# Work moved across the stage borders of a hybrid attention, state-space and expert layer: w_out split and step-size tables in the projections, the first head loaded there, one tile of mixing prepared instead of four

## The reference, cut to what matters

```
proj = x @ w_in                       # q k v | z | xs B C | dt, x: 1536 tokens x 1024
q, k = partial_rotary(q), partial_rotary(k)
attn = merge of dilated window attentions, by their log-sum-exps
xBC  = silu(centred_dwconv(xs B C))
dt   = softplus(dt + dt_bias); A = -exp(a_log)       # two directions, 8 heads each
y    = ssd_scan forward + ssd_scan backward + d_skip * xs
y    = rms_norm(y * silu(z)) * ssm_norm_w
x    = layer_norm(ALPHA * x + concat([attn, y]) @ w_out)
x    = layer_norm(ALPHA * x + expert_choice_ffn(x))  # 16 experts
```

## Time and profile before

| | us |
|---|---|
| median of 3 runs | 3694.23 (3691.44 to 3696.48) |
| the profiled execution | 3689.45 |
| its span, first to last instruction | 3687.6 |
| PE busy in it | 3435.1 |
| DVE, ACT, POOL busy | 2331.2, 1893.5, 409.3 |
| mean granted TensorE clock | 0.96 of full speed |

### The profile page before, as it was taken

How to read it: one execution, slowest core, us unless ns; L and a number is a source line. 1 busy time by engine, 2 the same in 40 slices (tenths; PEclk the granted TensorE clock), 3 DMA queues, 4 the chain that set the end, 5 groups by cost and what they waited for, 6 DMA issues and landing times. The chain is left out here.

```text
span 3687.6 us, 61850 instructions
## 1 busy us (share of the span) xinstructions
PE 3435.1 (93%) x20358; PEld 3124.9 (85%) x20358; DVE 2331.2 (63%) x3830; ACT 1893.5 (51%) x3320; POOL 409.3 (11%) x373
## 2 busy tenths in 40 slices
PE   8999699788939999999999999999999999999993
PEld 6888699566829899998989999898998989899992
DVE  6421067687657676666757667675776767667674
ACT  3222167342316565555656556565565656556564
POOL 0011064333200000000000000000000000000003
PEclk9999889898969999999999999999999999999997
DMA  4222353133327777767777777777777777677775
GB/s 165 77 66 74 85 143 99 43 110 110 128 75 233 236 230 236 237 213 232 235 222 233 234 235 221 235 235 218 236 230 221 232 239 235 217 234 224 237 234 184
DMA packets 240063, 699.41 MB, mean 190 GB/s; under 512 B 52960, under 2 KB 68608, under 8 KB 239520
## 3 DMA queue, kind: packets, MB, share of 16 engines
q1 hardware_dynamic: 225920, 648.13, 54.9%
q0 software_dynamic: 13056, 45.29, 4.8%
q10 hardware_dynamic: 864, 3.15, 0.2%
HBM read 642.89 MB, written 57.77 MB: 190 GB/s over the span
## 5 line engine op out<-in xcount | busy, mean ns | idle before, releaser
L1847 PE MATMUL moe_gu<-moe_xgT,moe_whi 128*128 128x384 f32 x5632 | 1634.4, 364 | 7.6 <-issue 3.6
L1979 DVE TENSOR_TENSOR moe_wlo<-moe_raw,moe_whi 128x1024 fp32r<-128x1024 f32 x1056 | 1290.3, 1223 | 484.0 <-ACT moe_whi L1933 483.4
L1848 PE MATMUL moe_gu<-moe_xgT,moe_wlo 128*128 128x192 f32 x5632 | 1414.1, 251 | 0.0
L1933 ACT CAST moe_whi<-moe_raw 128x1024 fp32r<-128x1024 f32 x1056 | 1106.1, 1048 | 443.9 <-PE moe_dnp L1863 389.1
L1848 PEld LDWEIGHTS moe_gu<-moe_xgT,moe_wlo 128*128 128x128 f32 x5632 | 1083.7, 192 | 0.4
L1847 PEld LDWEIGHTS moe_gu<-moe_xgT,moe_whi 128*128 128x128 f32 x5632 | 1065.2, 189 | 13.0 <-issue 4.9
L1940 ACT COPY moe_part<-moe_gu 128x384 f32<-128x384 f32 x352 | 168.7, 479 | 459.2 <-PE moe_gu L1848 459.2
L1985 DVE TENSOR_TENSOR moe_guv<-moe_gu,moe_part 128x384 f32<-128x384 f32 x352 | 196.3, 558 | 292.5 <-ACT moe_part L1940 292.5
L1812 POOL DMA_INDIRECT tmp_acc<-moe_og_s,moe_srow_s x16 | 25.7, 1608 | 2286.4 <-ACT moe_og_s L1965 2286.4
L1859 PE MATMUL moe_dns<-moe_whi,moe_hid 128*128 128x512 f32 x704 | 275.9, 392 | 0.0
L1862 PE MATMUL moe_dnp<-moe_whi,moe_hid 128*128 128x512 f32 x704 | 275.6, 392 | 0.0
(11 more groups left out here) (275 smaller groups left out, 4128.6 us busy)
## 6 DMA issues: line engine op xcount, KB each, us to landing
moe_raw<-in_w_ffn SPq DMA_DIRECT2D x1056, 512.0 KB, 4.1
prj_wraw<-in_w_in SPq DMA_DIRECT2D x12, 1024.0 KB, 5.4
att_raw<-tmp_qkT SPq DMA_DIRECT2D x32, 384.0 KB, 7.0
prj_share<-in_xT SPq DMA_DIRECT2D x6, 1024.0 KB, 10.4
tmp_qkT<-prj_share POOLq DMA_DIRECT2D x24, 256.0 KB, 2.7
ssd_xb<-tmp_xbc SPq DMA_DIRECT2D x12, 512.0 KB, 3.9
mix_rows<-in_x SPq DMA_DIRECT2D x12, 512.0 KB, 5.2
tmp_h<-mix_rows SPq DMA_DIRECT2D x12, 512.0 KB, 2.6
```

The source lines that it names most:

```text
L1847: pe.matmul(out[:, a, 0:2 * CAP], whi[c][:, j, :], x, start=(j == 0), stop=False)
L1848: mm = pe.matmul(out[:, a, 0:CAP], wlo[c][:, j, :], x[:, 0:CAP], start=False, stop=(j == KD - 1))
L1933: act.copy(whi[c][:], raw[c][:]).then_inc(hi_done, 1)
L1979: dve.tensor_tensor(wlo[c][:], raw[c][:], whi[c][:].bitcast(F32), ALU.subtract).then_inc(lo_done, 1)
```

## The change

In the projections Z becomes slice 4 and V slice 5. In the Z slice w_out is read in 16 parts of 128x512, split into a high and a low half by ACT and DVE, and both halves are stored to DRAM by SP; during the V slice the step-size tables are made; head 0's q and k are loaded into a tensor that all four stages share (`early`), in place of the weights' staging buffer. Attention gets head 0 from there: POOL copies k, ACT copies q and makes qc, DVE does both subtractions, and the DRAM copy of w_out is gone. The state-space stage starts its loop after three constants, and loads the high half of w_out at its end. Mixing loads the low half by eight transfers, has no splits of w_out, and prepares tile 0 alone before the first product; `gate`, `far` and `norm` run two tiles ahead, `backward` three, and `project` is cut into two halves with the next tile's `turn` between them.

```diff
-    XB, QK, V, Z = (0, 1), (2, 3), 4, 5
+    XB, QK, Z, V = (0, 1), (2, 3), 4, 5
+    def out_part(of, q):
+        k, n = q // (D // OUT_W), q % (D // OUT_W)
+        return of[P * k:P * k + P, OUT_W * n:OUT_W * n + OUT_W]
+    def out_parts(t):
+        return [q for q in (2 * t - 6, 2 * t - 5) if 0 <= q < OUT_PARTS]
+        wraw = res["early"][:, 0:KD * ZW].rearrange("p (k n) -> p k n", k=KD)
+        raw0 = res["early"][:, 0:2 * TOK].rearrange("p (n t) -> p n t", n=2)
+        wst = [m.sb(f"wst{s}", [P, OUT_W]) for s in range(2)]
+        osh = m.sb("osh", [P, OUT_W], F32R)
+        osl = m.sb("osl", [P, OUT_W], F32R)
```

SP in the projections, behind its last load of weights:

```diff
+            def out_load(q):
+                if q < OUT_PARTS:
+                    sp.dma_start(wst[q % 2][:], out_part(dram["w_out"], q)).then_inc(wst_in[q % 2], 16)
+            out_load(0)
+            out_load(1)
+            for q in range(OUT_PARTS):
+                sp.wait_ge(out_lo, q + 1)
+                sp.dma_start(out_part(dram["whi"], q), osh[:].bitcast(F32)).then_inc(out_out, 16)
+                sp.dma_start(out_part(dram["wlo"], q), osl[:].bitcast(F32)).then_inc(out_out, 16)
+                out_load(q + 2)
+            sp.wait_ge(w_lo, KD * NW)
+            for s in range(2):
+                sp.wait_ge(rows_out[s], 16 * NT + 16)
+            for n in range(2):
+                for half in range(2):
+                    sp.dma_start(raw0[HD * half:HD * half + HD, n, :], dram["qkT"][n * AW:n * AW + HD, :]).then_inc(raw0_in, 16)
```

PE in the projections:

```diff
+            def sums():
+                pe.wait_ge(const_in, 96)
+                pe.wait_ge(qkT_ready, 2 * NT)
+                pe.wait_ge(tables, 1)
+                for n, (of, off) in enumerate(((GT, 0), (LT, HEADS), (LE, 0), (GE, HEADS), (ONE, 0), (ONE, HEADS))):
+                    at = NT * HEADS * (n % 3)
+                    mm = pe.matmul(ps[:, BANKS + n // 3, at:at + NT * HEADS], tri[:, of, :], dtA[:, :, off:off + HEADS],
+                                   start=True, stop=True)
+                mm.then_inc(sums_mm, 1)
+                    if n == V and t == 6:
+                        sums()
```

ACT in the projections:

```diff
+            def out_high(q):
+                act.wait_ge(wst_in[q % 2], 16 * (q // 2) + 16)
+                if q:
+                    act.wait_ge(out_out, 32 * q)
+                act.copy(osh[:], wst[q % 2][:]).then_inc(out_hi, 1)
             for n in range(2, NW):
                 for t in range(NT):
-                    if n < Z and t == NT - 1:
+                    if n < NW - 1 and t == NT - 1:
                         for k in range(KD):
                             w_part(n + 1, k)
                     rows(n, t, 0)
...
                     if n == Z:
                         rows(n, t, 1)
+                        for q in out_parts(t):
+                            out_high(q)
+                    if n == V and t in (0, 1, 7):
+                        exponents(t)
```

DVE in the projections:

```diff
+            def out_low(q):
+                dve.wait_ge(out_hi, q + 1)
+                dve.tensor_tensor(osl[:], wst[q % 2][:], osh[:].bitcast(F32), ALU.subtract).then_inc(out_lo, 1)
...
+            steps()
```

POOL in the projections, behind its three constants:

```diff
+            for to, name in ((tri, "tri"), (dtb, "dt_bias"), (alog, "a_log")):
+                pool.dma_start(to[:], dram[name]).then_inc(const_in, 16)
```

SP, POOL, DVE and ACT in attention:

```diff
-                    for n in range(2):
+                    for n in range(2 if h else 0):
...
-                    if h == 2:
-                        sp.dma_start(dram["wout"], dram["w_out"]).then_inc(wout_out, 16)
...
+            pool.wait_ge(pads, len(ends))
+            pool.tensor_copy(k2[0][:, :, KR:KR + RUN], by_class(raw[0][:, 1, :])).then_inc(k0_hi, 1)
+            pool.wait_ge(k0_hi, 1)
+            for s in range(2):
+                pool.wait_ge(pads, len(ends) + s)
+                pool.memset(vn[s][:, ::NT, :], 0.0).then_inc(pads, 1)
             split(1, 0, 1)
...
+            dve.wait_ge(q0_hi, 1)
+            dve.tensor_tensor(q2[0][HD:, :], raw[0][HD:, 0, :], q2[0][HD:, :].bitcast(F32), ALU.subtract).then_inc(q0_lo, 1)
+            dve.wait_ge(k0_hi, 1)
+            dve.wait_ge(pads, 2)
+            dve.tensor_tensor(klo[0][:, :, KR:KR + RUN], by_class(raw[0][:, 1, :]), k2[0][:, :, KR:KR + RUN].bitcast(F32), ALU.subtract).then_inc(split_done, 1)
...
+            act.copy(q2[0][:], raw[0][:, 0, :]).then_inc(q0_hi, 1)
+            act.wait_ge(q0_lo, 1)
+            act.copy(qc[0][:], by_class(q2[0][:])).then_inc(split_done, 1)
```

The state-space stage:

```diff
-            for dst, name in ((tri, "tri"), (ident, "ident"), (dtb, "dt_bias"), (alog, "a_log"), (dsk, "d_skip")):
+            for dst, name in ((tri, "tri"), (ident, "ident"), (dsk, "d_skip")):
...
-            sp.dma_start(res["wlo"][:].bitcast(F32), dram["wout"].rearrange("(k p) n -> p k n", p=P)).then_inc(wout_in, 16)
+            sp.dma_start(res["whi"][:].bitcast(F32), dram["whi"].rearrange("(k p) n -> p k n", p=P)).then_inc(wout_in, 16)
```

SP in mixing:

```diff
             sp.dma_start(ml[:], dram["ml"].rearrange("(t p) f -> p t f", p=P)).then_inc(ml_in, 16)
-            load_c(1)
             load_gate(0)
             load_far(0)
-            load_c(2)
+            sp.dma_start(normw[:], dram["norm_w"]).then_inc(normw_in, 16)
+            sp.dma_start(ident[:], dram["ident"]).then_inc(ident_in, 16)
+            load_c(1)
             load_gate(1)
...
             load_far(1)
+            for k in range(KD):
+                sp.dma_start(wlo[:, k, :].bitcast(F32), wlo_src[:, k, :]).then_inc(wlo_in[k], 16)
+                if k == 1:
+                    load_c(2)
             load_x(0)
```

PE in mixing:

```diff
-            for n in range(-4, NT + 1):
+            backward(1)
+            turn(0)
+            for n in range(NT + 1):
+                project(n, 0)
                 turn(n + 1)
-                project(n)
+                if n == 0:
+                    backward(2)
+                project(n, 1)
                 turn_rows(n - 1)
-                backward(n + 4)
+                backward(n + 3)
                 route(n - 1)
```

DVE in mixing:

```diff
             weights()
+            far(0)
             dve.wait_ge(normw_in, 16)
-            dve.wait_ge(wide_ready, 1)
-            for n in range(-4, NT + 1):
+            norm(0)
+            low(0, 0)
+            low(0, 1)
+            backward(1)
+            gate(1)
+            far(1)
+            norm(1)
+            backward(2)
+            low(1, 0)
+            for n in range(NT + 1):
```

More of the change, by code:

```diff
@@ L474, in stage_attend @@
         m = Mem(nc, ctx, "att")
-        raw = [m.sb(f"raw{s}", [P, 2, TOK]) for s in range(2)]
+        raw = [res["early"][:, 0:2 * TOK].rearrange("p (n t) -> p n t", n=2), m.sb("raw1", [P, 2, TOK])]
         q2 = [m.sb(f"q2{s}", [P, TOK], F32R) for s in range(2)]
@@ L579, in _ @@
                 pool.memset(gaps.bitcast(F32), 0.0).then_inc(pads, 1)
-            for s in range(2):
-                pool.wait_ge(pads, len(ends) + s)
-                pool.memset(vn[s][:, ::NT, :], 0.0).then_inc(pads, 1)
             def split(h, hh, s):
@@ L866, in _ @@
                 pe.sem_inc(sem, n)
[L867 to L875 removed]
+            pe.wait_ge(const_in, 48)
             def to_tokens(t, tt, s):
@@ L1131, in stage_mix @@
         m = Mem(nc, ctx, "mix")
-        whi = m.sb("whi", [P, KD, D], F32R)
-        wlo = res["wlo"]
+        whi = res["whi"]
+        wlo = m.sb("wlo", [P, KD, D], F32R)
         wr = m.sb("wr", [P, KD, EXPERTS])
@@ L1138, in stage_mix @@
         half = m.sb("half", [P, 1])
-        rows = [m.sb(f"rows{s}", [P, D]) for s in range(ROWS)]
-        junk = m.sb("junk", [P, D])
+        rows = [res["early"][:, D * s:D * s + D] for s in range(ROWS)]
+        junk = res["early"][:, D * ROWS:D * ROWS + D]
         ss = m.sb("ss", [P, NT])
@@ L1275, in _ @@
             load_x(1)
-            for n in range(-3, NT):
-                load_c(n + 6)
-                load_gate(n + 5)
-                load_far(n + 5)
+            for n in range(-1, NT):
+                load_c(n + 4)
+                load_gate(n + 3)
+                load_far(n + 3)
                 if n >= 0:
@@ L1415, in squares @@
                     act.wait_ge(squared, i)
-                if i >= 3:
-                    act.wait_ge(var_ready, i - 2)
+                if i >= 2:
+                    act.wait_ge(var_ready, i - 1)
                 act.activation(junk[:, 0:SSM_W], y[:, tile(i), :], ACT.Square, accum_out=ss[:, i:i + 1]).then_inc(squared, 1)
-            def weights(k):
-                act.copy(whi[:, k, :], wlo[:, k, :].bitcast(F32)).then_inc(whi_ready, 1)
             for i in range(2):
@@ L1425, in _ @@
                 act.activation(ex[i][:], ex[i][:], ACT.Exp).then_inc(merge_exp, 1)
-            for k in range(4):
-                weights(k)
-            for n in range(-3, NT + 1):
+            squares(0)
+            high(0, 0)
+            high(0, 1)
+            squares(1)
+            high(1, 0)
+            for n in range(NT + 1):
                 high(n + 1, 1)
@@ L2140, in residents_state @@
     return {
-        "ex": m.sb("ex", [P, 6, NT, HEADS]),
```

(2 more changed lines are left out.)

293 lines of the change are left out of this document (151 added, 142 removed).

## The result

The changed kernel took 3667.86 us (median of 4 runs, 3662.12 to 3669.59) beside 3695.36 for the kernel before (4 runs): ratio 0.9925, 95% interval 0.9913 to 0.9938, 0.75% faster. The profiled execution took 3669.14 us, span 3667.3, so 20.3 us less span than before.

The account below looks back on a forecast made before the run. TensorE, busy 93% of the span, was taken as the bound, two thirds of that in the untouched experts' loop. Gains of 12 + 12.4 + 19 less 31.5 lost make 12 us, so 3682 us, range 3650 to 3700.

Parts of the forecast that it names:

- the likeliest case: Whole kernel: the forecast itself, 12 us gained to 3682 us, own range 3671 to 3694; chance 0.60.
- Step 1: Projections: splitting w_out in the Z slice makes PE wait before V; 31.5 us lost (23 to 48).
- the turn: Z slice: one w_out part's copy, subtraction and stores until the landing, 4.6 us (4.1 to 5.7), sixteen parts in one chain.
- Step 2: Attention: first head loaded early and the w_out copy's stall removed; 12 us gained (8 to 18).
- the copy's stall: Attention, ahead of head 3: loads queued behind the w_out copy; stall with its slow stretch cost about 13 us, removed.
- the slow stretch: Attention, after head 1's stall: clock falls for 7.6 to 19 us, costing 3.5 to 8 us.
- Step 3: State-space stage: the chain to the step-size tables goes, so segments start earlier; 12.4 us gained (11 to 14).
- Step 4: Mixing: first product 22.9 us earlier, part given back to later waits; 19 us gained (14 to 22).
- two thirds of that is the experts' loop, which the diff leaves alone: Experts: two thirds of TensorE's busy time, untouched by the diff; change of 0 us forecast.
- The dear split: Rival, projections: slower stores, landing 5.0 and turn 6.8 us, stall 33 us longer, 3715 us; chance 0.14.
- The free split: Rival, projections: PE never waits for V's weights, needing a turn of 3 us; 3653 us; chance 0.12.
- the opening given back: Rival, attention: head 1's load lands late, stall and long slow stretch both come; gains 5, not 12; 3689 us; chance 0.14.

Follow-up runs that it names:

- double_buffer: Changed kernel with two pairs of buffers for the split of w_out, so a copy waits for the stores two parts back: 3638.18 us, ratio 0.9852.
- copy_early: Kernel before, with the DRAM copy of w_out issued at the end of the projections' queue instead of in the attention: 3682.63 us, ratio 0.9966.
- earlier_both: double_buffer plus w_out's parts split two tiles earlier and head 1's loads issued ahead of head 0's values: 3624.35 us, ratio 0.9816.
- the padded kernels before: Kernel before with idle ScalarE instructions (1, 4, 11, 22, 64 or 254) ahead of the experts' loop: ratios 0.9940 to 0.9960.
- pad_before: Kernel before with 22 idle instructions (met waits) on ScalarE at the start of the experts: 3678.43 us, ratio 0.9952.
- 254: Kernel before with 254 idle ScalarE instructions in the stage that chooses the experts' tokens: 3674.66 us, ratio 0.9956.
- shift 0: ScalarE's experts' code unmoved from its place in the kernel before, as in that kernel itself: 3695.36 us.
- 1 and 11: Kernel before with 1 or 11 idle ScalarE instructions at the start of the experts: 3674.04 us (ratio 0.9940) and 3676.90 us (0.9960).
- shift 4: Kernel before with 4 idle ScalarE instructions at the start of the experts: 3680.28 us, ratio 0.9948.

## Why the prediction was right, and where it was not

The median, 3667.9, lies in the range on record (3650 to 3700) and on the side that had 0.64, but below the likeliest case's own range (3671 to 3694), and what carried it there was not in the sum. That it fell on the fast side is chance: about 17 of the 27.5 us gained come from where ScalarE's code happened to lie (below).

**Step 1, projections: mechanism right, the landing mis-sized.** Of "the turn is 4.6 us (4.1 to 5.7)" the measured value is 5.06, all of it in the landing: 3.33 us in the mean for the 2.8 taken, and 4.5 to 5.0 in three of the turns, where copies "a steady 4.6 us apart" were forecast. Why some landings are longer no run shows; the first copy stood at 317.7 (318.2 forecast). Fifteen turns make 0.46 into 6.9 us, and V's first product comes at 395.7, 31.8 after the 363.9 at which PE would have finished Z (25 forecast; 387.2 in the forecast is moreover the start of the sixteenth copy and not its end, 0.6 us). Behind V's first product the clock was 0.50 for 4.3 us (395.7 to 400.0) and 0.96 after it, a loss of about 2 where 4 were forecast, and the products of the tables took 1.5 as forecast. "Six PSUM banks cover the late evictions till about then" was wrong: 6.3 us of PE's waiting came in two pieces before Z's end. That changes where the waiting shows, not its sum: the chain sets the end. That the chain's landing is the cause is shown by double_buffer, 25.2 us back. The estimate of a turn of 5.5 us, worked out from the Trainium skill's table (DMA: Bandwidth & Descriptors, "Latency and other measured facts" and "Bandwidth"), missed by as much above as mine did below.

**Step 2, attention: the sum right, by two terms that offset.** -13.3 for -12. The copy's stall was 10.8 us (13 forecast; copy_early). First scores came 13.1 us earlier, not 15, since DVE subtracts for q (4.18 us) ahead of klo (2.88), and my sum had only klo's. What counts for the sum is when head 1 can start: 37.9 us after the stage's first issue for 42.8 before, 4.9 earlier (5.2 forecast). Its stall was 3.7 us (5.7 forecast), and after it the clock was 0.53 for 14 us (forecast: between 7.6 and 19). So the copy's stall gave about 2 less than forecast, and the slow stretch took about 2 where 6 were allowed; these differences are of the size of the scatter. The stall and the slow stretch follow from the order of the loads, as earlier_both shows: with head 1 first the stall is gone and attention 9.8 us shorter. By the Trainium skill's rule (TensorE: Matmul & The Clock Gate, "What's actually happening") activity should have released the throttle early; the 14 us of a fully busy PE at 0.53 don't agree.

**Step 3, state space: right.** Segments 12.6 us earlier in the stage (12.4 forecast), the stage 12.1 shorter.

**Step 4, mixing: right at its start, a little less at its end.** The first product is 23.1 us earlier in the stage (22.9 forecast). Of this 5.8 us are given back later, 3.9 forecast; I didn't follow the difference: it is within the scatter of this stage, and the means of ten and four kernels give the 19.0 of the forecast.

**The experts: the step that failed is "two thirds of that is the experts' loop, which the diff leaves alone".** The loop's text is the same, but the diff adds 22 instructions to ScalarE ahead of it, and the place they pushed it to is worth 13 us of the 20 in the profile. By runs: the padded kernels before lie at ratios 0.994 to 0.996, the changed one at 0.9925, so with ScalarE's code in an equal place (pad_before, 0.9952) the change itself is worth about 0.0027 of 3695, 10 us (2 to 18 by the two intervals), and the other 17 or so of the medians' 27.5 are the place. The forecast's 12 described the edits well. It missed more than half of the total, which nothing in it weighed: that an edit can move the code of a loop and so change its time.

**The rivals.** The dear split (0.14) had the right direction, a turn above 4.6, but needed 5.9 to decide. The free split (0.12) was out. For the opening given back (0.14) attention would have gained 5; it gained 13.3.

## What stays open

Why the place matters is argued, not shown. The Trainium skill (Runtime: NRT & Kernel Launch, "Instruction fetch mechanics") has an engine hold two blocks of 256 instructions, and a taken branch out of them wait for a fetch. The loop spans 356 of ScalarE's instructions, counted in the program, so it lies in two blocks or in three, by its place. At 254, two short of a whole block, no return waits; at 0 all six do. A border just ahead of the loop's last instruction at shift 0 would make both: a return that just fits, and one that has just left its block. That is one free number fitted to two runs after the fact, it doesn't say why 4 (2.6 to 4.8 us) is worse than 1 and 11, and no run set out to test it. The profile of shift 4 is moreover of its slowest execution (3686.49 us, median 3680.28), so its 3.5 us may be long for that kernel. Shown is only: the same code, moved by idle instructions, returns in 0, 2.3 to 2.8 or 3.5 us, and unmoved in 4.3 to 4.6.

## What to carry to other kernels

A single buffer in a chain that ends in a store to device memory costs its landing at every turn, with all that stands behind it on the engine: count turns times landing, and give it a second buffer from space that is idle then (25 us here). When an engine is freed early, ask which load it wants next and issue that one first: the early head gave hardly anything (2.5 us, within the scatter) until head 1's loads went ahead of head 0's values, and then 9.8 more. And before a difference of half a per cent is put down to an edit, look at the loops that the edit moves: a kernel with a long loop needs a control whose instruction streams are moved by nothing but idle instructions.

## What the runs showed of the hardware

- ScalarE's return to the start of a loop of 356 instructions took none to 4.6 us (mean of six) by the place of its code alone; the seven kernels with a moved loop and otherwise the code of before were 0.4 to 0.6% faster.
- In the experts' loop PE stalls of 2.0 to 2.6 us were followed by 11.6 us at a mean granted clock of 0.71 or 0.72 (four of five; 0.85 in one), stalls of 0.5 to 1.6 us by 0.85 (six of seven), and one of 0.99 us by 1.00. The two experts around them took 316.4 us (1429.7 to 1746.1) in the kernel before and 312.5 (1423.0 to 1735.5) in the changed one: 3.9 us for 1.5 us more of standing at the first return.
- The copy of w_out, 4096 KB read and written, cost nothing in the projections (439.4 for 439.3 us) and 10.8 us in the attention, ahead of loads that were wanted soon (one execution each).
- A store of 256 KB behind another of 256 KB landed 2.4 to 5.0 us after its issue, 3.33 in the mean of 15, in one chain of the changed kernel.
